# Output projection, two feed-forwards and the convolution's input in one block of a Trainium2 kernel, with the three norms between them worked on in token halves

## The reference

```python
# layer 0, behind attention a_lat and gating b_lat
y_lat = jnp.concatenate([a_lat, b_lat], axis=-1) @ w_out
lat = residual(lat, y_lat, m_lat, 1, ln_g[0, 1], ln_b[0, 1], 1.0)                  # n01
lat = ffn_sublayer(lat, m_lat, 2, ffn_w13[0, 1], ffn_w2[0, 1], ln_g[0, 2], ln_b[0, 2])   # f01, n02
# layer 1
lat = ffn_sublayer(lat, m_lat, 0, ffn_w13[1, 0], ffn_w2[1, 0], ln_g[1, 0], ln_b[1, 0])   # f10, n10
h_lat = modulate(lat, m_lat, 1)
a, gt = jnp.split(h_lat @ w_pw1 + b_pw1, 2, axis=-1)                               # c_in
y = a * jax.nn.sigmoid(gt)                                                         # to the depthwise convolution

def modulate(h, mod, idx):
    return h * (1 + mod[:, 3 * idx + 1][:, None]) + mod[:, 3 * idx][:, None]
def residual(h, y, mod, idx, g, b, weight):
    return layer_norm(ALPHA * h + weight * mod[:, 3 * idx + 2][:, None] * y, g, b)
def swiglu(h, w13, w2):
    gt, up = jnp.split(h @ w13, 2, axis=-1)
    return (jax.nn.silu(gt) * up) @ w2
def ffn_sublayer(h, mod, idx, w13, w2, g, b):
    return residual(h, swiglu(modulate(h, mod, idx), w13, w2), mod, idx, g, b, MACARON)
```

## Time and profile before

| what | us |
|---|---|
| median of 3 runs (lowest to highest) | 3964.05 (3961.94 to 3966.99) |
| the profiled execution, its own time | 3964.17 |
| span of its trace | 3962.4 |
| TensorE busy (share) | 3648.7 (92%) |
| VectorE busy (share) | 2168.9 (55%) |
| ScalarE busy (share) | 1504.4 (38%) |
| GpSimd busy (share) | 357.0 (9%) |
| mean granted clock of TensorE, 1 being 2.4 GHz | 0.957 |

### The profile page before, as it was taken

One profiled execution on the slowest core, in us unless ns is written; L12 is line 12 of the kernel. 1 busy time (PEld: TensorE's weight loads), 2 busy tenths in 40 slices (PEclk: granted clock), 3 DMA queues, 4 the chain that ended last, 5 costly groups with the idle time before them and its releaser, 6 DMA issues. The chain is left out here.

```text
span 3962.4 us, 43441 instructions
## 1 busy us (share of the span) xinstructions
PE 3648.7 (92%) x16746; PEld 2871.5 (72%) x16746; DVE 2168.9 (55%) x2770; ACT 1504.4 (38%) x1698; POOL 357.0 (9%) x269
## 2 busy tenths in 40 slices
PE   7999997999799999997986999789898998999996
PEld 6888885744588888885735888567787776878785
DVE  6545356345544466555385333345325434999996
ACT  4212113323422232223234222344445424777774
POOL 2000000000100001001001000000000001443432
PEclk9999998989899999998998999899999998999998
DMA  6322232110144325443101322130221224999996
GB/s 239 116 96 96 96 109 79 59 32 1 60 142 138 122 80 191 162 155 97 65 0 54 107 95 88 41 110 11 96 86 54 86 77 168 357 355 351 354 371 247
DMA packets 314985, 519.34 MB, mean 131 GB/s; under 512 B 19748, under 2 KB 274513, under 8 KB 289104
## 3 DMA queue, kind: packets, MB, share of 16 engines
q1 hardware_dynamic: 304944, 508.48, 37.2%
q0 software_dynamic: 9888, 8.72, 0.7%
HBM read 519.23 MB, written 23.07 MB: 137 GB/s over the span
## 5 line engine op out<-in xcount | busy, mean ns | idle before, releaser
L547 PE MATMUL banks<-f_h_hi,f_weights_hi 128*128 128x512 f32 (+1 forms) x1056 | 320.1, 357 | 18.4 <-DVE f_h_lo L794 13.5
L547 PE MATMUL banks<-f_h_hi,f_weights_lo 128*128 128x512 f32 (+1 forms) x1056 | 320.7, 358 | 0.0
L547 PE MATMUL banks<-f_h_lo,f_weights_hi 128*128 128x512 f32 (+1 forms) x1056 | 318.5, 356 | 0.0
L3326 DVE TENSOR_TENSOR ex_w_lo<-weight_ring,ex_w_hi 128x2048 fp32r<-128x2048 f32 x128 | 288.7, 2291 | 41.7 <-ACT ex_w_hi L3261 41.7
L547 PE MATMUL banks<-pair_h_hi,pair_weights_hi 128*128 128x512 f32 (+1 forms) x736 | 284.7, 387 | 24.5 <-DVE pair_h_lo L1360 12.1
L547 PE MATMUL banks<-pair_h_hi,pair_weights_lo 128*128 128x512 f32 (+1 forms) x736 | 281.7, 383 | 0.0
L547 PE MATMUL banks<-pair_h_lo,pair_weights_hi 128*128 128x512 f32 (+1 forms) x736 | 281.6, 383 | 0.0
L3261 ACT ACTIVATE ex_w_hi<-weight_ring 128x2048 fp32r<-128x2048 f32 x128 | 241.7, 1913 | 21.6 <-PE banks L3176 21.6
L724 DVE TENSOR_TENSOR f_weights_lo<-weight_ring,f_weights_hi 128x2048 fp32r<-128x2048 f32 (+1 forms) x68 | 152.0, 2236 | 137.1 <-ACT f_weights_hi L683 133.8
L3176 PE MATMUL banks<-ex_w_hi,ex_x_hi 128*128 128x512 f32 x512 | 209.8, 410 | 9.6 <-DVE ex_x_lo L3330 5.8
L683 ACT ACTIVATE f_weights_hi<-weight_ring 128x2048 fp32r<-128x2048 f32 (+1 forms) x68 | 126.4, 1859 | 228.0 <-PE banks L547 225.2
(11 more groups left out here) (566 smaller groups left out, 8103.5 us busy)
## 6 DMA issues: line engine op xcount, KB each, us to landing
weight_ring<-ffn_w SPq DMA_DIRECT2D x120, 1024.0 KB, 5.3
weight_ring<-w_mod SPq DMA_DIRECT2D x72, 1024.0 KB, 5.1
weight_ring<-w_gate SPq DMA_DIRECT2D x64, 1024.0 KB, 5.9
weight_ring<-w_up SPq DMA_DIRECT2D x64, 1024.0 KB, 7.2
mixed_branches<-w_down SPq DMA_DIRECT2D x64, 1024.0 KB, 7.2
weight_ring<-w_in SPq DMA_DIRECT2D x26, 1024.0 KB, 5.2
weight_ring<-ffn_w SPq DMA_DIRECT2D x16, 768.0 KB, 5.0
weight_ring<-o_w_pw SPq DMA_DIRECT2D x8, 1024.0 KB, 5.4
```

The source lines that it names most:

```text
L547: ins = pe.matmul(bank[:, at:at + width], w, x[:, at:at + width], start=start and n == 0, stop=stop and n == len(passes) - 1)
L3326: dve.tensor_tensor(w_lo[:, c % 3, :], raw[c], w_hi[:, c % 3, :].bitcast(F32), ALU.subtract).then_inc(s_lo, count)
```

## The change

One function, `trunk`, takes the place of the output projection, of `n01`, of `ffn_pair`, of `n10` and of the convolution's input. It is one block. In it:

- The output projection is the new class `Projection`. Its first chunk is split in two pieces, interleaved with the split of its input, and its first two output tiles are computed together, feature tile by feature tile, over all 512 tokens (`pe_first`). The other 6 tiles are computed in halves of 256 tokens, first all of half 0, then all of half 1 (`pe_rest`).
- `n01` and `n10` become objects of `Boundary`, as n02 was. A new class `Crossing` holds the lists of the engines at such a boundary, so all three share one order. This order differs from that of n02 before in two places: the split of the following stage's chunk 1 comes behind `sweep(0)`, and the second variance stands in the middle of head part (half 0, chunk 1).
- The last down projection of f10 is cut in halves (the tail), as that of f01 was. f01 now has a head in four parts like f10.
- The convolution's input is the new class `GatedInput`, with the same head in four parts; the other 6 chunks are of full width.
- The first group of f01 is written out instead of standing in a loop. In it and in the convolution's input DVE and GpSimd complete `k.X` (`dve_rescale`, `pool_keep`), with the bias of the convolution's output folded in for n10, so that `c_out` needs no scaling by GpSimd any more.
- Of the two `renew_semaphores`, the one between n01 and the first feed-forward moves in front of the output projection, and the one behind f10 moves behind the convolution's input.

```diff
-def ffn_pair(k, norm, between):
+class Projection:
...
+    PIECES = 2
+    REGION = (2, 0, 1, 2)
...
+    def pe_first(self, pe, nb):
+        hi, lo = (wide(self.region(w, 0)) for w in (self.w_hi, self.w_lo))
+        for kk in range(KD):
+            pe.wait_ge(self.s_lo, kk * self.PIECES // KD + 1)
+            pe.wait_ge(self.s_xlo, kk + 1)
+            for x in range(2):
+                bank = self.k.PS[0][:, 512 * x:512 * x + S]
+                w_hi, w_lo = (w[:, kk, x * P:(x + 1) * P] for w in (hi, lo))
+                pe.matmul(bank, w_hi, self.x_hi[:, kk, :], start=kk == 0, stop=False)
+                pe.matmul(bank, w_hi, self.x_lo[:, kk, :], start=False, stop=False)
...
+    def pe_rest(self, pe, nb, during):
+        for u in range(2):
+            for x in range(2, KD):
+                c, b = divmod(x, 2)
+                hi, lo = (wide(self.region(w, c)) for w in (self.w_hi, self.w_lo))
+                pe.wait_ge(self.s_lo, self.PIECES + c)
+                if x >= 3:
+                    pe.wait_ge(nb.added[u], x - 2)
...
+                    during(u, x, kk)
...
+class Crossing:
...
+    def pe_in_tail(self, pe, u, x, kk):
+        if (u, x, kk) == (1, self.first, self.mean_at):
+            self.nb.pe_mean(pe, 0)
+        if (u, x, kk) == (1, self.var_tile, self.var_at):
+            self.nb.pe_var(pe, 0)
+
+    def pe_head(self, pe):
+        def during(u, c, kk):
+            if (u, c, kk) == (0, 0, 3):
+                self.nb.pe_mean(pe, 1)
+            if (u, c, kk) == (0, 1, 3):
+                self.nb.pe_var(pe, 1)
+        self.following.pe_head(pe, self.nb, during)
...
+    def dve(self, dve, prepare=lambda: None):
...
+        for x in range(self.first, 4):
+            self.dve_add(dve, 0, x)
+        prepare()
+        for x in range(4, KD):
+            self.dve_add(dve, 0, x)
+        nb.dve_last_sum(dve, 0, self.order[0])
+        second(adds["mean"])
+        centre(0, lambda kk: second(adds["centre"].get(kk, ())))
+        second(adds["var"])
+        nb.dve_rs(dve, 0)
+        following.dve_lo(dve, 0, 0, FG)
+        sweep(0, lambda kk: second(adds["sweep"].get(kk, ())))
+        following.dve_lo(dve, 0, 1, FG)
+        centre(1)
+        nb.dve_rs(dve, 1)
+        sweep(1)
...
+def trunk(k, room):
...
+        to_one = Crossing(n01, gate(0, 1), by_m, lambda u, x: out.bank(n01, u, x), one, first=2, sums=(4, 4, 6),
+                          adds=dict(mean=[], centre={4: [2]}, var=[3], sweep={0: [4], 1: [5], 2: [6], 4: [7]}))
+        to_two = Crossing(n02, gate(0, 2), by_tail, n02.bank, two)
+        to_conv = Crossing(n10, gate(1, 0), by_tail, n10.bank, conv)
...
         @block.tensor
         def _(pe):
-            with pe.Fori(0, FGS) as i:
-                one.pe_group(pe, i, FG, lambda kk: pe.wait_ge(one.s_xlo, kk + 1))
...
+            out.pe_first(pe, n01)
+            out.pe_rest(pe, n01, lambda u, x, kk: to_one.pe_in_tail(pe, u, x, kk))
+            to_one.pe_head(pe)
             for c in range(2, FG + 4):
-                two.pe_chunk(pe, 0, FG, c)
-            with pe.Fori(1, FGS) as i:
-                two.pe_group(pe, i, FG)
-            two.pe_group(pe, FGS, FREST)
+                one.pe_chunk(pe, 0, FG, c)
+            for stage, over in ((one, to_two), (two, to_conv)):
...
+                stage.pe_tail(pe, over.nb, in_tail)
+                over.pe_head(pe)
...
+            for c in range(2, 8):
+                conv.pe_chunk(pe, c)
...
-def residual_stage(k, name, rhs, gate, bias=None):
+def residual_stage(k, name, rhs, gate):
...
-        def scale_x(pool, s):
-            for kk in range(KD):
-                ins = pool.tensor_scalar(k.X[:, kk, 0:S], k.X[:, kk, 0:S], ALPHA, 0.0 if bias is None else bias(kk), ALU.mult, ALU.add)
-            ins.then_inc(s.pool, 1)
...
-            norm_stage(k, "n01", k.X, S, KD, D, LN_EPS, *ln(0, 1), summed=True, keep_rstd=True)
-            k.renew_semaphores()
...
-            ffn_pair(k, ln(0, 1), [k.col[:, at:at + KD] for at in gain])
-            k.renew_semaphores()
...
-            norm_stage(k, "n10", k.X, S, KD, D, LN_EPS, *ln(1, 0), then=(1, 1, LAT), summed=True)
-            conv_mixer(k)
+            conv_mixer(k, room)
```

534 lines of the change are left out of this document (305 added, 229 removed).

## The result

The changed kernel takes 3920.91 us (median of 4 runs, 3917.64 to 3925.91), the kernel before 3964.45 us beside it: ratio 0.9891, 95% interval 0.9874 to 0.9908. A second measurement gave 3924.29 against 3963.05 us, 0.9902 (0.9886 to 0.9919). The forecast was 3922 us, 42.4 us less; measured are 43.5 and 38.8 us less.

What follows compares the result with a forecast made beforehand. TensorE bounds the kernel, standing still for VectorE at the norms worked on whole. Savings 4.0 + 16.4 + 22.0 = 42.4 us from 3964.2 give 3922 us; own range 3913 to 3931, with partial overlap 3911 to 3942.

Steps and rivals of the forecast that it cites:

- The bound: Whole kernel: TensorE, busy 92%, sets the time; it stands still at n01 and n10, waiting for VectorE's last operand split.
- n02 as the pattern: At n01 and n10: same work and cover as n02, so each head ends at t0 + 50.7 us.
- n02, 4.0 us: At n02: moving chunk 1's split and issuing the second variance earlier saves 4.0 us, between 2 and 5.
- the case of its lower end, 2 us: At n02: only the wait's part is saved, some eaten by the variance waiting in order with 15 products behind it.
- Output projection and n01, 16.4 us: Output projection, n01 and start of f01: chunks 0 and 1 done at 1080.9, not 1097.3; 16.4 us saved, between 13 and 18.
- the first product at 999.4: Output projection's start: splitting the first chunk in two pieces brings the first product to 999.4, before at 1000.68, despite +1.3 for renewal.
- n10, 22.0 us: f10's tail, n10, convolution's input: gain 23.3 less 1.3 for the renewal, so 22.0 us, between 18 and 24.
- a wait for a bank: In f10's tail 1.3 us was included; TensorE waiting for a bank, VectorE late at the adds, would show the forecast wrong.
- The halves: Half-width products at the boundaries: 0.0135 us more per pair, 6.5 us for 480 pairs, inside the intervals.
- The clock rival: At the three boundaries: waits drop the clock, about 40 us lost, 3962 us, no change; chance 0.06.
- cost at nothing: Completing `k.X` beside later chunks, GpSimd's dropped scaling and later ring slots: taken as 0 us.
- Partial overlap: At the two new boundaries: VectorE's in-order list costs 5 to 10 us each, 15 in all, 3937 us; chance 0.15.

Runs made afterwards that it cites:

- the cover taken away: Changed kernel, with TensorE finishing half 1's second mean, variance and last low part before the next stage's 192 half-width products, at all three boundaries: 3978.23 us.
- the experiment with the variance: Kernel before, only n02's second variance moved from behind the eighth feature tile to behind the fourth: tail's start to head's end 68.04 us, before 72.70.

## Why the prediction was right, step by step

- **The bound.** Right: TensorE stood still for VectorE at n01 and n10, and most of the gain is that idle time. With the cover taken away (57 us) the kernel falls behind the one before. What the prediction didn't name is that the norms' own products on TensorE became fewer as well.
- **n02 as the pattern.** The interval from half 1's start to the head's end was forecast as 50.7 us at all three places. Counting 15 products back from the mean at n01 and 12 at the others, it is 49.1, 50.5 and 50.1 us.
- **n02, 4.0 us.** Size right, working half right. The variance did come about 3 us earlier (it starts 31.6 us behind the first mean, 34.5 before). TensorE now waits 2.35 us for the variance's input, with the rest of the part behind it. The prediction had named this as the case of its lower end, 2 us; yet 4.3 were saved. It gave the split's place nothing; alone it is worth 2.6 us, half of it by the clock. It comes out as nothing only since the variance's place already takes the same slack. And the part for products at half clock was 1.8 us in the experiment with the variance, not 1.0.
- **Output projection and n01, 16.4 us; measured 15.8** (15.7 to 18.2 over the traces). The step that failed is the first product at 999.4, 7.3 us behind the start of the attention's last products. It came 8.4 us behind it, because VectorE computes n01's columns first (996.89 to 998.5). They stand in the list ahead of the split, and the prediction didn't count them. The first two tiles took another 1.1 us more than forecast in this trace (13.7 us, forecast 12.6), with a clock of 0.64 over the first 8 us. The head's interval was 1.6 us shorter. So the head ended 88.4 us behind the attention's last products (87.3 to 88.4 in five traces), forecast 87.9: errors of 1 to 2 us that cancel, which is luck. The working of 999.4 has two sizes that aren't in its rows: half of 1.91 and half of 2.28 are 2.1 us, not 1.15 + 1.4. Measured are 2.3: from ScalarE's first conversion to the first product it is 5.69 us before and 3.37 with the columns moved. And the renewal costs 1.0 us there, not 1.3 (from the attention's last product to ScalarE's first conversion 0.9 us before, 1.9 now).
- **n10, 22.0 us; measured 21.2** (19.6 to 21.3 over the traces). Half 0's tail took 20.9 us (1783.13 to 1805.50 - 1.44), forecast 19.95; the two stalls for VectorE's modulation sums and for the bank are there (0.79 and 0.87). The prediction had set down a wait for a bank as a sign of being wrong and 1.3 us for one in its sum; it came, and was too short to matter. The head's interval was 0.6 us shorter. The renewal cost 1.6 (3.24 instead of 1.60), not 1.3.
- **The halves.** 0.0132 us per pair against 0.0135: the term of 6.5 us stands. The rule of the Trainium skill (TensorE: Matmul & The Clock Gate, Back-to-back issue gap) for isolated products, 2.5 ns per pair, doesn't hold for these.
- **The clock rival.** Clock 0.97, 0.98 and 1.00 over the boundaries. Filling the wait at the variance changed nothing, so this rival is out. What the prediction cost at nothing and what was not always nothing is the clock behind the boundary. The moved renewal makes the pause in front of the depthwise convolution longer, and the clock fell behind it in five of eight traces, for 0.8 or 1.9 us. The rest of the profiled execution's 2.5 us is the norm behind it (34.3 us to the convolution's output, 33.7 before), where the two kernels' other traces overlap (34.5 to 34.9 and 33.9 to 35.1).
- **Partial overlap.** The longest wait in a head is 2.36 us, forecast at most 2; no wait of 5 us stands anywhere in a tail or head, and none makes up the rival's 5 to 10 us per boundary.
- **The range.** The ends of the three terms add up to 33 and 47 us, so to 3917 to 3931 and not to 3913; the result lies in either.

What stays open is the whole time to better than about 3 us: the two measurements differ by 4.8 us in the gain, with intervals of some 13 us; the traces give 39.0 and 40.2 us.

## What to carry to other kernels

Work a norm's boundary in token halves when the products on each side are long enough to cover the other half's chain; an interval measured at one such boundary forecast two others to within 2 us. When two edits aim at one wait, they don't add: find which engine is late for the event, and price both by that. Behind such a change look for small setup work (columns, semaphores) that now stands on the path, but measure what it is worth at the end of the stretch and not where it stands (1.2 us at the first product were 0.2 to 1.3 at the head's end). Read the clock of the next stage too, in more than one trace.

## Not expected of the hardware

- After the same pause of 3.24 us TensorE's clock over the next 8 us was 0.64 and 0.65 in two executions, 0.79 in three and 1.00 in three; after one of 1.60 or 1.62 us it was 1.00 in all six traces. Up to the norm behind it this is 100.4, 99.3 and 98.5 us. What decides between them isn't settled.
- An executed program's early part moves by up to 7 us between executions (986.5 to 993.7 us for the same event), while distances of 48 us behind it repeat within 0.1 us where the clock is the same.
